# First layers of a two-model kernel: input and forget gates projected between k and v, their chain run beside v, output gates in two parts, and the convolution two tiles at a time

## The reference, cut to what matters

```python
z = h @ w_in + b_in            # q, k, v of attention; mq, mk, mv, mo of the mLSTM; mi, mf; ga, gb
aq, ak = apply_partial_rope(aq, cos, sin), apply_partial_rope(ak, cos, sin)
ya = dilated_mixture_attention(aq, ak, av)
qk = silu(causal_short_conv(z[..., COL_MQ:COL_MV], conv_w, conv_b))   # 4 taps, 1024 channels
hm = mlstm_chunkwise(mq, mk, mv, mi, mf)
hm = hm * rsqrt(mean(hm * hm)) * mlstm_norm_w
yb = sigmoid(z[..., COL_MO:COL_MI]) * hm
mixed = sigmoid(ga) * (ya @ w_proj_att) + sigmoid(gb) * (yb @ w_proj_mlstm)
x = x + mixed @ w_out
x = x + square(relu(rms_norm(x) @ w_ff1)) @ w_ff2
```

## Time and profile before

| | |
|---|---|
| median of 3 runs | 2585.06 us (2582.84 to 2586.93) |
| the profiled execution | 2585.52 us |
| its span, first to last instruction | 2583.7 us |
| TensorE busy in it | 2485.9 us (96%) |
| VectorE, ACT, POOL busy | 995.9, 871.4, 1115.9 us |
| mean granted clock of TensorE | 0.983 of full |

### The profile page before, as it was taken

One profiled execution on the slowest core, in us unless ns is written; L12 is line 12 of the kernel. 1 busy time (PEld: TensorE's weight loads), 2 busy tenths in 40 slices (PEclk: granted clock), 3 DMA queues, 4 the chain that ended last, 5 costly groups with the idle time before them and its releaser, 6 DMA issues.

```text
span 2583.7 us, 30118 instructions
## 1 busy us (share of the span) xinstructions
PE 2485.9 (96%) x11731; PEld 2008.2 (78%) x11731; DVE 995.9 (39%) x1578; ACT 871.4 (34%) x1090; POOL 1115.9 (43%) x808
## 2 busy tenths in 40 slices
PE   6999999999999999999999999899898799999998
PEld 5867788888888867788888887688675588888887
DVE  4456543311203455644211203638485424322201
ACT  4254333422324254333421313432324323322213
POOL 3433345554544433344554544622242245455543
PEclk9999999999999999999999999988899999999999
DMA  4212123222223222223322222220222123323221
GB/s 134 83 52 79 49 90 99 89 98 98 98 98 102 66 66 66 66 82 98 98 98 95 96 100 86 67 66 25 64 73 66 54 82 98 98 97 97 97 98 65
DMA packets 174011, 215.16 MB, mean 83 GB/s; under 512 B 7644, under 2 KB 155028, under 8 KB 173908
## 3 DMA queue, kind: packets, MB, share of 16 engines
q1 hardware_dynamic: 171236, 209.81, 25.1%
q10 hardware_dynamic: 2672, 3.89, 0.4%
HBM read 211.19 MB, written 2.10 MB: 83 GB/s over the span
## 4 chain that ended last, share of the span: by engine, by line
issue 47%; POOL 28%; PE 23%; DVE 1%; ACT 0%; POOLq 0%; DVEq 0%; ACTq 0%
POOL w_lo L276 28%; PE ps L707 6%; PE ps L306 3%; PE ps L308 3%; PE ps L307 3%; PE ps L1705 2%; PE ps L1703 2%; PE ps L1701 2%; PE ps L832 0%; PE ps L857 0%; PE ps L844 0%; PE ps L2269 0%; POOLq L278 0%; ACT att_probsT L925 0%; DVE s_window L2296 0%
## 5 line engine op out<-in xcount | busy, mean ns | idle before, releaser
L276 POOL TENSOR_TENSOR w_lo<-w_raw,w_hi 128x512 fp32r<-128x512 f32 x804 | 1115.7, 1419 | 1441.1 <-ACT w_hi L267 1441.1
L267 ACT ACTIVATE w_hi<-w_raw 128x2048 fp32r<-128x2048 f32 x201 | 384.8, 1915 | 1069.1 <-PE ps L308 393.2
L707 PE MATMUL ps<-h_hi,w_hi 128*128 128x512 f32 (+1 forms) x936 | 399.8, 427 | 11.2 <-POOL w_lo L276 6.2
L707 PE MATMUL ps<-h_hi,w_lo 128*128 128x512 f32 (+1 forms) x936 | 372.0, 397 | 0.0
L707 PE MATMUL ps<-h_lo,w_hi 128*128 128x512 f32 (+1 forms) x936 | 371.2, 397 | 0.0
L306 PE MATMUL ps<-h_hi,w_hi 128*128 128x512 f32 x816 | 319.0, 391 | 0.0
L308 PE MATMUL ps<-h_hi,w_lo 128*128 128x512 f32 x816 | 317.5, 389 | 0.0
L307 PE MATMUL ps<-h_lo,w_hi 128*128 128x512 f32 x816 | 317.4, 389 | 0.0
L707 PEld LDWEIGHTS ps<-h_hi,w_hi 128*128 128x128 f32 (+1 forms) x936 | 177.6, 190 | 79.3 <-issue 32.7
L707 PEld LDWEIGHTS ps<-h_lo,w_hi 128*128 128x128 f32 (+1 forms) x936 | 177.8, 190 | 44.1 <-issue 8.6
L707 PEld LDWEIGHTS ps<-h_hi,w_lo 128*128 128x128 f32 (+1 forms) x936 | 177.0, 189 | 42.2
(11 more groups left out here) (399 smaller groups left out, 3686.6 us busy)
## 6 DMA issues: line engine op xcount, KB each, us to landing
w_raw<-in_w_in SPq DMA_DIRECT2D x72, 1024.0 KB, 5.2
w_raw<-in_w_ff SPq DMA_DIRECT2D x64, 1024.0 KB, 5.1
w_raw<-in_w_ffn_in SPq DMA_DIRECT2D x22, 1024.0 KB, 5.1
w_raw<-in_w_out SPq DMA_DIRECT2D x12, 1024.0 KB, 5.0
w_raw<-in_w_ffn_out SPq DMA_DIRECT2D x11, 1024.0 KB, 4.9
w_raw<-in_w_proj_att SPq DMA_DIRECT2D x4, 1024.0 KB, 5.0
w_raw<-in_w_proj_mlstm SPq DMA_DIRECT2D x4, 1024.0 KB, 5.0
w_raw<-in_w_up_ssd SPq DMA_DIRECT2D x4, 1024.0 KB, 5.7
```

The costliest lines, as they stand in the source:

```text
L267: act.activation(k.whi[:, slot * SLOT:(slot + 1) * SLOT], k.wraw[:, slot * SLOT:(slot + 1) * SLOT], ACT.Copy).then_inc(k.hi_done, 1)
L276: ins = pool.tensor_tensor(k.wlo[:, a:a + T], k.wraw[:, a:a + T], k.whi[:, a:a + T], ALU.subtract)
L707: mm = pe.matmul(out, lhs, rhs, start=i == 0 and n == 0, stop=stop and n == 2)
```

## The change

The small gate unit moves from behind the convolution's input to between k and v. Its chain (Turn, Softplus, Gates) now runs beside v, ahead of Rope, with 2 + 5 + 9 pieces; all nine of Gates stand ahead of the wait for the scan. The running maxima go to a tile of their own, `k.gm`. The output gates' two units are parted: the first stays behind mv, the second comes after the first gate and projection of the attention branch. Conv takes two tiles at a time on ACT and VectorE, waits tile by tile for its input (`ready`), and stands directly ahead of Mlstm. Mlstm puts side pieces between its four spread matmuls (`AHEAD`). Budgets change.

```diff
-BESIDE1 = {"rope": 11, "att": 38, "conv": 15, "forget": 5, "gates": 7, "mlstm": 42}
+BESIDE1 = {"turn": 2, "forget": 5, "gates": 9, "rope": 14, "att": 40, "conv": 16, "mlstm": 54}
...
 class Conv(Stage):
+    def ready(self, t):
+        job = self.jobs[t]
+        return self.side.posted(job) if job.post else self.side.read(job)
+
+    def come(self, who, eng, p):
+        self.side_out(who, eng, p, self.tiles + 2)
+        if self.jobs and p < self.tiles:
+            self.side.emit_out(who, eng, self.jobs[p + 1].end)
+
     def act(self, act):
         k = self.k
         self.join(act)
-        for t in range(self.tiles):
-            if t % 4 == 0:
-                self.side_out("act", act, t // 4 * 3, self.tiles // 4 * 3)
-            act.activation(self.dst[:, t * T:(t + 1) * T], self.tap(t, 0), ACT.Identity,
-                           bias=k.col(self.bcol + t), scale=k.col(self.wcol + t))\
-               .then_inc(self.sem("tap"), 1)
-        for t in range(self.tiles):
-            self.side_out("act", act, t + self.tiles, 2 * self.tiles)
-            act.wait_ge(*self.at("taps", t + 1))
-            d = self.dst[:, t * T:(t + 1) * T]
-            act.activation(d, d, ACT.Silu).then_inc(self.sem("silu"), 1)
+        for p in range(0, self.tiles + 2, 2):
+            self.come("act", act, p)
+            for t in range(p, min(p + 2, self.tiles)):
+                if self.jobs:
+                    act.wait_ge(*self.ready(t))
+                act.activation(self.dst[:, t * T:(t + 1) * T], self.tap(t, 0), ACT.Identity,
+                               bias=k.col(self.bcol + t), scale=k.col(self.wcol + t))\
+                   .then_inc(self.sem("tap"), 1)
+            for t in range(max(p - 2, 0), p):
+                act.wait_ge(*self.at("taps", t + 1))
+                d = self.dst[:, t * T:(t + 1) * T]
+                act.activation(d, d, ACT.Silu).then_inc(self.sem("silu"), 1)
 
     def dve(self, dve):
         k = self.k
         self.join(dve)
-        for t0 in range(0, self.tiles, 4):
+        for p in range(0, self.tiles, 2):
+            self.come("dve", dve, p)
             for j in range(1, CONV):
-                self.side_out("dve", dve, t0 // 4 * 3 + j - 1, self.tiles // 4 * 3)
-                for t in range(t0, t0 + 4):
+                for t in range(p, p + 2):
...
+            self.side_out("dve", dve, p + 1, self.tiles + 2)
+        self.side_out("dve", dve, 1, 1)
...
 class Gates(Stage):
         tr.then_inc(self.sem("rows"), 1)
-        self.side_pe(pe, 0, 2)
+        self.side_pe(pe, 0, 1)
         pe.wait_ge(*self.at("scan", 6))
...
         tr.then_inc(self.sem("cols"), 1)
-        self.side_pe(pe, 1, 2)
...
 class Mlstm(Stage):
+    AHEAD = MH
...
-        self.steps = MH * (TT + 1) + MH + 4
+        self.steps = self.AHEAD + MH * (TT + 1) + MH + 4
...
-            pe.matmul(k.ps[:, 4 + h, :], k.pick(h, MH), k.gr[0:MH, 3 * T:4 * T], start=True, stop=True)\
+            pe.matmul(k.ps[:, 4 + h, :], k.pick(h, MH), k.gm[0:MH, :], start=True, stop=True)\
               .then_inc(self.sem("spread"), 1)
+            self.side_pe(pe, step, self.steps)
+            step += 1
...
 def first_layer(k, l, A, st, before, angles):
+    rest = add(Rest, "to_gates", side, gates_at + BESIDE1["turn"], gates_at, prev=[])
+    at = gates_at + BESIDE1["turn"]
     add(Turn, "turn", grows, 0, 8, gate_out)
...
+    at = att.beside(side, at, BESIDE1["att"])
+    conv = Conv(k, "conv", [att], cv, mqk, 8, c0 + CW, c0 + CB, cv_jobs)
+    conv.settle()
+    st.append(conv)
+    at = conv.beside(side, at, BESIDE1["conv"])
+    mlstm = Mlstm(k, "mlstm", [conv], mqk, mv, mo, [], o_scr, o_v, *yb, c0 + MN)
+    gate(0, 0, att.ends)
+    up(0, 0, att.ends, conv.ends)
+    plain(MO + UC, UC, [out_gate(2, [mlstm.at("spread", MH)]), out_gate(3)])
+    mlstm.mo_ready = [side.posted(side.jobs[-1])]
```

More of the change, by code:

```diff
@@ L1093, in dve @@
         self.side_out("dve", dve, 0, 2)
-        b, ig, a, m = (k.gr[0:MH, i * T:(i + 1) * T] for i in range(4))
+        b, ig, a = (k.gr[0:MH, i * T:(i + 1) * T] for i in range(3))
+        m = k.gm[0:MH, :]
         s = self.sem("scan")
@@ L1227, in dve @@
             if h == 0:
+                self.side_out("dve", dve, self.AHEAD, self.steps)
                 dve.wait_ge(*self.at("maxima", MH))
@@ L1232, in dve @@
             for s in range(TT):
[L1233 removed]
+                self.side_out("dve", dve, self.AHEAD + h * (TT + 1) + s, self.steps)
                 if s + 1 < TT:
@@ L2658, in first_layer, with tiles, gate, up @@
     for j in range(2):
-        values_at = plain(MV + j * UC, UC, [values(j, 0), values(j, 1)])
-    for j in range(2):
-        plain(MO + j * UC, UC, [out_gate(2 * j), out_gate(2 * j + 1)])
-    mo_ready = [side.posted(side.jobs[-1])]
+        qkv_at = plain(AV + j * UC, UC, [att_values(j, 0), att_values(j, 1)])
+    for j in range(4):
+        plain(MQ + j * UC, UC, [conv_in(2 * j), conv_in(2 * j + 1)])
+    cv_jobs = side.jobs[-8:]
+    for j in range(2):
+        values_at = plain(MV + j * UC, UC, [values(j, 0), values(j, 1)])
+    plain(MO, UC, [out_gate(0), out_gate(1)])
+    def tiles(x):
+        return lambda i: x[:, i * T:(i + 1) * T]
+    def gate(n, half, free):
+        gcol, b0 = ((GA, 4), (GB, 12))[n]
+        side.gate(lambda c: weight(w_in, l, 0, D, gcol + c, UC), half,
+                  bias=lambda t: k.hbias[:, l * 20 + b0 + t:l * 20 + b0 + t + 1], free=free)
+    def up(n, half, need, free):
+        w, y = (("w_proj_att", ya), ("w_proj_mlstm", yb))[n]
+        side.up(lambda c, cols: weight(A[w], l, 0, 512, c, cols), 4, (tiles(y[0]), tiles(y[1])), half, n > 0,
+                need=need, free=free)
     if l == 0:
@@ L2692, in first_layer, with head @@
     at = gates.beside(side, at, BESIDE1["gates"])
-    rest = add(Rest, "to_mlstm", side, values_at)
-    mlstm = add(Mlstm, "mlstm", mqk, mv, mo, mo_ready, o_scr, o_v, *yb, c0 + MN)
-    at = mlstm.beside(side, at, BESIDE1["mlstm"])
-    for n, (b0, gcol, w, y, need) in enumerate(((4, GA, "w_proj_att", ya, att), (12, GB, "w_proj_mlstm", yb, mlstm))):
-        for half in range(2):
-            side.gate(lambda c, gcol=gcol: weight(w_in, l, 0, D, gcol + c, UC), half,
-                      bias=lambda t, b0=b0: k.hbias[:, l * 20 + b0 + t:l * 20 + b0 + t + 1], free=att.ends)
-            side.up(lambda c, cols, w=w: weight(A[w], l, 0, 512, c, cols), 4, (tiles(y[0]), tiles(y[1])), half,
-                    n > 0, need=need.ends if half == 0 else (), free=conv.ends)
-    side.settle()
+    rest = add(Rest, "to_rope", side, max(at, qkv_at))
+    t1, t2 = k.at("rope_cos", o_scr, 2 * T), k.at("rope_sin", o_scr + 2 * T, 2 * T)
+    rope = add(Rope, "rope", qk, t1, t2, prev=[rest, st[2]] if l == 0 else [rest])
+    at = rope.beside(side, max(at, qkv_at), BESIDE1["rope"])
+    def head(x, t0):
+        return lambda h: x[h % 2 * HD:(h % 2 + 1) * HD, (t0 + h // 2) * T:(t0 + h // 2 + 1) * T]
+    att = add(Attention, "att", head(qk, 0), head(qk, 4), lambda b, h: v[:, b * 512 + h * HD:b * 512 + (h + 1) * HD],
+              lambda i: k.cst[:, C_PAT + (TT - 1 - i) * P:C_PAT + TT * P], o_scr, o_mo, *ya,
+              bias=lambda p: k.col(c0 + B1 + 8 + p))
+    at = att.beside(side, at, BESIDE1["att"])
[8 more added lines that the diff above has]
+    mlstm.mo_ready = [side.posted(side.jobs[-1])]
+    gate(0, 1, ())
+    up(0, 1, (), ())
+    gate(1, 0, ())
+    up(1, 0, mlstm.ends, ())
+    gate(1, 1, ())
+    up(1, 1, (), ())
+    side.settle()
+    assert at >= values_at
+    mlstm.settle()
+    st.append(mlstm)
+    at = mlstm.beside(side, at, BESIDE1["mlstm"])
     mix = [k.at(f"mixed_{p}", at, 4096, F32R) for at, p in ((o_ya, "hi"), (o_v, "lo"))]
```

58 lines of the change are left out of this document (21 added, 37 removed).

## The result

| | before | with the change |
|---|---|---|
| median | 2584.53 us (11 runs) | 2591.37 us (11 runs, 2588.13 to 2596.57) |
| ratio | | 1.0025, 95% interval 1.0017 to 1.0033 |
| the profiled execution | 2585.52 us | 2594.51 us |
| its span | 2583.7 us | 2592.7 us |

The change makes the kernel slower, by 6.8 us. The forecast was 2584.6 us and no change; the time lies within the range given, but on the side to which the forecast gave 0.28.

A forecast was written before the change was run, and what follows sets the result against it. TensorE's own work, waits and half clock bound the kernel; 22.2 us coming against 22.7 going gave 2585.0 us from the profiled 2585.52, written as a median of 2584.6 us, no change, with an 8 in 10 range of 2572 to 2597.

The forecast's parts named there:

- idle time that goes: First two layers: TensorE's waits for POOL's weight splits, Gates' scan, Mlstm's maxima and Turn disappear, 11.9 us.
- gate unit, v waits for POOL: Between k and v: the short gate unit leaves v's weight split uncovered, 1.6 us a layer, 3.2 us.
- Rope's join: Rope's start: VectorE's copy or ScalarE's table load and exponential come late, 2.0 us instead of 1.12, 1.8 us in all.
- Mlstm waits for the last silu: Mlstm's first spread matmul waits for the end of Conv, 4.4 us a layer, 8.8 in both.
- half clock, gone and come: First two layers: 10.8 us of half-clock loss goes; 4.8 comes behind Mlstm's waits and 1.6 at Rope's join.
- third layer: Third layer's Conv: POOL's second split may get in on VectorE's last pair; 2.0 us, ends 0 and 4.1.
- The conv chain: First layers' Conv: VectorE's steps, evacuations, ScalarE round trips and POOL outlast 16 side pieces, a 4.4 us wait a layer.
- rival (d): Conv: POOL is let in after each VectorE step, +2.1 in the third layer, +3 in each other; 2593 us, chance 0.06.
- Rival (c): Conv: both splits meet VectorE's steps, TensorE waits 8.6 us at Mlstm, clock falls as often; 2599 us, chance 0.22.
- rival (e): Rope's join: ScalarE's table load adds a drain of some 1.38 us; 2587 us, chance 0.03.
- The clock: First two layers: half-clock loss of 10.8 us goes, and 4.8 at Mlstm and 1.6 at Rope come.

The follow-up runs named there:

- e1: The change with attention at 38 side pieces instead of 40 and Rope at 16 instead of 14; 2585.17 us, ratio 1.0001 to the kernel before.
- Experiments 1 and 2: The change with attention 38 and Rope 16 pieces, 2585.17 us; the kernel before with attention 40 and Conv 13 pieces, 2597.79 us.
- e6: e5 with Conv's first taps ahead of the preceding split and the last two silus ahead of the gate's tanh; 2571.18 us, ratio 0.9942.
- e9: e6 with seven side pieces ahead of Gates' wait for the scan and two behind its transposes, instead of nine ahead; 2566.16 us, ratio 0.9930.
- e7: e1 with the third layer's Conv as before the change, in blocks of four tiles; 2583.66 us, ratio 0.9998.
- e5: e1 with ScalarE issuing the next pair's first taps ahead of the tanh in the first layers' Conv; 2578.76 us, ratio 0.9977.

## Why the prediction was right and where it was wrong

Its own terms, against the profiled execution with the change (both layers together):

| term | predicted | measured |
|---|---|---|
| idle time that goes | 11.9 | 11.9 |
| gate unit, v waits for POOL | 3.2 | 3.3 (1.64 at 85.94 and at 861.13) |
| Rope's join | +1.8 | +1.5 (1.82 twice, for 1.12 and 0.98) |
| Mlstm waits for the last silu | 8.8 | 8.3 (4.15, 4.17) |
| attention | not in the sum | +3.3 |
| half clock, gone and come | -10.8 + 6.4 | +1.7 |
| TensorE busy longer outside half clock | not in the sum | +2.3 |
| third layer | +2.0 | +0.5 (2.9 at Turn, given back behind it) |
| sum | -0.5 | +9.0 |

Half clock is taken as half of TensorE's busy time in its stretches, 28.7 us now and 25.3 before; the row under it is what is left of the busy time.

**What failed** is a step that was not there. The budget of attention went from 38 to 40 in the part on the change; the prediction looked at the pieces beside Conv, Mlstm and Gates and named attention only as a stage "which I leave alone", so that the sum has it at nothing. Measured are 3.3 us more of waits in the two layers (7.3 us at L857 instead of 2.0, less 2.0 that went at two other lines of attention), and 6.2 us of time by `e1`. It should have run the 57 slots through `share`: the kernel before has three waits of 0.3 to 0.4 us at L857 in the first layer although every slot between the halves holds a piece, so that an empty slot had to show. The prediction had named the sign for it, waits in attention that were not there before, and it was the first thing that the list of waits showed. Experiments 1 and 2 show the mechanism in both kernels, from both sides. Taken out, the change measures 2585.17 us, against the 2584.6 forecast; 6.2 of the 6.8 us are this term. That the two agree so closely is in part luck: in the profile of `e1` the first two layers are 3.4 us shorter than before, where the sum has 2.5, and the third is 3.6 us longer, where it has 2.0.

**The conv chain** was right in its pieces. VectorE began 0.2 us behind TensorE's first piece, two gaps of 1.50 us came from ScalarE's tanh and first tap (1.6 were taken), and POOL's split cost the second pair 2.9 us (2.6 were taken). Two sums in it are not exact: 16 x 1.37 is 21.9, and 24.1 with a tanh and two silus is 25.9, so that its own figures give a wait of 4.0 us, not 4.4; 4.15 was measured. VectorE's timeline of the changed kernel:

```profile
235.59 4.07 DVE L984 SCALAR_TENSOR_TENSOR conv_out<-conv_in,all_param_cols,conv_out 128x512 f32<-128x512 f32 x6 [1.57 <-ACT conv_out L964]
239.57 0.69 DVE L2622 TENSOR_TENSOR mo<-ps,rstd 128x512 f32<-128x512 f32 x1
241.75 6.97 DVE L984 SCALAR_TENSOR_TENSOR conv_out<-conv_in,all_param_cols,conv_out 128x512 f32<-128x512 f32 x6 [1.50 <-ACT conv_out L964]
248.64 0.68 DVE L1356 TENSOR_TENSOR gate<-ps,rstd 128x512 f32<-128x512 f32 x1
250.82 8.09 DVE L984 SCALAR_TENSOR_TENSOR conv_out<-conv_in,all_param_cols,conv_out 128x512 f32<-128x512 f32 x12 [1.50 <-ACT conv_out L964]
258.82 1.29 DVE L1356 TENSOR_TENSOR gate<-ps,rstd 128x512 f32<-128x512 f32 x2
```

The next split came at 257.48, in the last two pairs. Their 12 steps, 8.09 us, ran at 0.67 each, and POOL's first instruction took 2.56 us instead of 1.27. So here rival (d) did not come: POOL was not let in after each step, as the earlier trace rows had suggested. In the third layer it was let in. POOL's split and VectorE's steps there:

```profile
1681.40 6.85 POOL L276 TENSOR_TENSOR w_lo<-w_raw,w_hi 128x512 fp32r<-128x512 f32 x4 [9.12 <-ACT w_hi L267]
...
1666.57 23.54 DVE L984 SCALAR_TENSOR_TENSOR s_conv_out<-s_conv_in,all_param_cols,s_conv_out 128x512 f32<-128x512 f32 x24
```

The split came 0.65 us ahead of the last pair, and four of that pair's six steps followed each other at 1.67 us instead of 0.67: 4.0 us, the upper end of the prediction's term (4.1) and what (d) says of this layer. `e1`, `e6` and `e9` show the same. The Trainium skill (SBUF — State Buffer, Who interferes with whom) has the first to issue hold the shared ports for its whole instruction while the other is blocked. The trace agrees with that in the third layer, where the two took turns at 1.67 us. In the first layer one POOL instruction was held over two of VectorE's, at 257.49 and 258.16, which goes beyond that rule. Rival (c) had its price from the chain of the first layers and did not come; the slowdown came from elsewhere.

**Rope's join** was right in mechanism: the copy at 111.24, the table load at 111.49, the exponential at 112.78, Rope at 113.02. The load took 1.28 us and the ACTIVATE stood right behind it, as in the earlier trace rows; the extra drain of rival (e) does not show.

**The clock** was mis-sized, by 6.1 us in the profiled execution. The prediction let 10.8 us go and 6.4 come, with the fall behind each long wait as the mean of two; measured is +1.7 where the sum has -4.4. One stretch, the one at 55.8, came without the change. Behind equal waits of 4.15 us half clock lasted 13.7 us in the change's first layer and 6.8 in its second, and 6.8 in both layers of `e1` and `e7`. In the profile of `e1` the first two layers' idle time is 0.1 us longer than before and half clock gives 4.2 us, near the 4.4 predicted. The busy time outside half clock is 2.3 us longer in the change and 0.8 in `e1`; no run takes it apart.

What the five empty slots did to the clock stays open. The 13.7 us stand in the first layer in both profiles of the change, but the second layer has the same empty slots and 6.8. In the first two layers the slots go with 12.1 us, 4.5 of them idle time, and in the third with 3.1 us less, so the 1.7 us of the medians (6.2 less 4.5) are no measure of their share.

**The third layer** cost 0.4 and 0.5 us in the two profiles of the change and 3.6 in `e1`, with the same code and the same waits. Of the 2.9 us at Turn 1.2 are idle time and the rest is half clock; how much of it is given back behind Turn is a matter of half clock too.

## What to carry to other kernels

Where a budget of filler work is spread over slots by rounding, a changed total moves the filler between slots. Compute which slots lose it, and look for the slot that covers a wait; two pieces more can cost more than they cover. And on an in-order queue, put what another engine's chain waits for ahead of what itself waits for that engine: that alone took the kernel from no difference to 14 us faster. What a wait is worth beyond its own length can't be counted on: in the first two layers `e6` got back 11.6 us for 8.3 of wait and `e9` 4.9 for 2.0, but `e5` only 3.8 for 5.2. And look where the time went: a stage that the edit does not touch can move by several us through the clock.
